# First expert's turned rows from an early gather of five token tiles and one-hot products for the other three

## The reference

```
x   = x + merged @ w_out
h2  = rms_norm(x, norm2_g)
gl  = h2 @ w_gr + b_gr                     # 4 groups
el  = h2 @ w_er + b_er                     # 4 x 8 experts
g   = argmax(gl);  top 2 of the 8 experts of group g
w   = softmax(top 2 logits) * softmax(gl)[g]
out = x + sum over the token's two experts of w * ((silu(h2 @ w_gate) * (h2 @ w_up)) @ w_down)
```

## Time and profile before

| | us |
|---|---|
| three runs, median (lowest to highest) | 1482.31 (1481.53 to 1482.49) |
| the profiled execution, its own time | 1481.47 |
| its span in the profile | 1479.7 |
| TensorE busy | 1424.3 (96%) |
| VectorE busy | 1008.1 (68%) |
| ScalarE busy | 828.9 (56%) |
| GpSimd busy | 407.7 (28%) |
| mean of a weight piece's high half on ScalarE | 1.907 |
| mean of a weight piece's low half on VectorE | 2.285 |

### The profile page before, as it was taken

The page is one execution under the profiler, slowest core; times in us unless marked ns, Lnnn a source line. Parts: engine busy times, 40 slices in busy tenths (PEclk is TensorE's granted clock), DMA queues, the critical chain, the costliest instruction groups (busy, mean ns, idle before and its releaser), DMA issues.

```text
span 1479.7 us, 19519 instructions
## 1 busy us (share of the span) xinstructions
PE 1424.3 (96%) x7296; PEld 1199.5 (81%) x7297; DVE 1008.1 (68%) x1444; ACT 828.9 (56%) x1342; POOL 407.7 (28%) x462
## 2 busy tenths in 40 slices
PE   5899999999999999999999979999999999999996
PEld 5788888888888788888888867888888888888885
DVE  6855664664574533344332567999999999999996
ACT  5653453353353322233232227888888888888883
POOL 3225424424433400000000011233333333333331
PEclk9999999999999999999999988999999999999999
DMA  7010110210210143354330549999999999999992
GB/s 220 23 44 12 51 44 1 62 43 1 61 44 0 44 115 99 86 149 121 91 142 36 198 152 385 375 386 385 392 386 387 386 389 389 393 396 393 389 384 89
DMA packets 134032, 286.39 MB, mean 194 GB/s; under 512 B 18864, under 2 KB 97840, under 8 KB 109360
## 3 DMA queue, kind: packets, MB, share of 16 engines
q1 hardware_dynamic: 119216, 263.79, 49.3%
q0 software_dynamic: 13248, 21.00, 3.8%
q10 hardware_dynamic: 1472, 0.32, 0.1%
HBM read 287.16 MB, written 25.17 MB: 211 GB/s over the span
## 4 chain that ended last, share of the span: by engine, by line
PE 85%; DMA 4%; DVE 4%; ACT 2%; POOL 2%; issue 2%; POOLq 0%; DVEq 0%; ACTq 0%
PE proj L105 17%; PE proj L107 16%; PE proj L106 16%; PE scores L105 6%; PE scores L107 6%; PE scores L106 6%; DMA w_slot<-in_w_up 4%; PE outs L760 2%; PE scores L693 2%; PE scores L571 1%; PE turned L105 1%; PE turned L107 1%; PE turned L106 1%; PE outs L851 1%; DVE w_low L1747 1%
## 5 line engine op out<-in xcount | busy, mean ns | idle before, releaser
L1747 DVE TENSOR_TENSOR w_low<-w_slot,w_high 128x2048 fp32r<-128x2048 f32 x192 | 430.9, 2285 | 0.1
L1186 ACT ACTIVATE w_high<-w_slot 128x2048 fp32r<-128x2048 f32 x190 | 352.6, 1907 | 20.1 <-DMA w_slot<-in_w_up 8.5
L105 PE MATMUL proj<-w_high,xeH 128*128 128x512 f32 x512 | 203.8, 398 | 3.9 <-DVE xeL L1850 1.9
L107 PE MATMUL proj<-w_high,xeL 128*128 128x512 f32 x512 | 200.6, 392 | 0.0
L106 PE MATMUL proj<-w_low,xeH 128*128 128x512 f32 x512 | 200.1, 391 | 0.0
L1376 POOL DMA_INDIRECT out<-y,ids_rows x31 | 86.5, 2791 | 342.8 <-DVE y L1860 342.8
L999 ACT ACTIVATE wCH<-wC_in 128x1024 fp32r<-128x1024 f32 x48 | 47.6, 1052 | 154.1 <-DMA wC_in<-in_w_branch_b 154.1
L1442 DVE TENSOR_TENSOR wCL<-wC_in,wCH 128x1024 fp32r<-128x1024 f32 x48 | 56.9, 1237 | 92.3 <-ACT wCH L999 92.3
L105 PEld LDWEIGHTS proj<-w_high,xeH 128*128 128x128 f32 x512 | 97.0, 189 | 25.5 <-issue 3.7
L107 PEld LDWEIGHTS proj<-w_high,xeL 128*128 128x128 f32 x512 | 96.5, 188 | 20.9
L106 PEld LDWEIGHTS proj<-w_low,xeH 128*128 128x128 f32 x512 | 96.7, 189 | 19.2
(11 more groups left out here) (299 smaller groups left out, 3167.4 us busy)
## 6 DMA issues: line engine op xcount, KB each, us to landing
w_slot<-in_w_gate SPq DMA_DIRECT2D x64, 1024.0 KB, 11.1
w_slot<-in_w_up SPq DMA_DIRECT2D x64, 1024.0 KB, 11.2
w_slot<-in_w_down SPq DMA_DIRECT2D x64, 1024.0 KB, 11.7
wC_in<-in_w_in SPq DMA_DIRECT2D x32, 512.0 KB, 4.8
wB_in<-in_w_in SPq DMA_DIRECT2D x16, 512.0 KB, 6.1
wA_in<-in_w_in SPq DMA_DIRECT2D x12, 512.0 KB, 5.9
x_all<-in_x SPq DMA_DIRECT2D x4, 1024.0 KB, 8.8
wC_in<-in_w_branch_a SPq DMA_DIRECT2D x16, 256.0 KB, 5.7
```

What stands on the lines that cost most here:

```text
L105: pe.matmul(out, lh, rh, start=start, stop=False)
L107: return pe.matmul(out, ll, rh, start=False, stop=stop)
L1186: act.activation(w_high[slot][:], w_in6[slot][:], ACT.Copy).then_inc(S["w_split"], 1)
L1747: dve.tensor_tensor(w_low[slot][:], w_in6[slot][:], w_high[slot][:].bitcast(F32), ALU.subtract).then_inc(S["w_lows"], 1)
```

## The change

Tiles 0 to 4 are "early" (`N_EARLY = 5`).

- The row table of tiles 0 to 4 is closed by itself and gives `first_ids`; GpSimd gathers expert 0's rows of these tiles into `xe[1]`, in its list ahead of the norm factor of tile 6. `rows_of(4)` moves ahead of the last piece of `out_proj(15)`.
- For tiles 5 to 7 VectorE makes a one-hot row for expert 0 alone (`first_hot`), and TensorE multiplies x2 with it. These products and products of the gathered rows with the identity add up in the banks 6 and 5, in which the turned rows of expert 0 then stand. They are interleaved with the last routing jobs.
- VectorE, not ScalarE, scales the turned rows; the high and low halves of the first four blocks are made one block at a time.
- The picks and row products of tiles 5 to 7 and the table `ids_rows` come later: the row products behind the first quarter of expert 0's gate and up. The gather of all of expert 0's rows (for the norm and the residual) and that of expert 1 follow this table.
- SP loads pieces 4 to 7 after the early gather has landed (`xe_landed1`), and 8 and on after the turned rows and all stores.
- Piece 2's high half is made by ScalarE after half tile 11, its low half by VectorE in iteration 4, in the projection stage.
- `top_group` is one step shorter; VectorE's places of tile 5 stand ahead of the last residual; the last result's scatter waits for one count instead of two; some waits on stores are merged.

```
 SP
-            sp.wait_ge(S["xe_landed0"], DMA)
+            sp.wait_ge(S["xe_landed1"], DMA)
             for q in range(4, 6 * N_EXP):
                 if q == 8:
-                    sp.wait_ge(S["x2_stored"], N_TILES * DMA)
-                    sp.wait_ge(S["out_stored"], N_TILES * DMA)
+                    sp.wait_ge(S["x0_T"], 2)
+                    sp.wait_ge(S["early_stored"], 2 * N_EARLY * DMA)
+                    sp.wait_ge(S["late_stored"], 2 * (N_TILES - N_EARLY) * DMA)
...
 TensorE, after out_proj(15)
+            def first_late(t, ks):
+                pe.wait_ge(S["place_step"], FIRST_HOT[t])
+                for k in ks:
+                    last = pe.matmul(first_turned(k), x2[:, t, DS(k, 128, step=8)], first_pick[t - N_EARLY][:, :],
+                                     start=(t == N_EARLY and k % 4 == 0), stop=(t == N_TILES - 1 and k % 4 == 3))
+                return last
+            def first_early(ks):
+                pe.wait_ge(S["xe_landed1"], DMA)
+                for k in ks:
+                    pe.matmul(first_turned(k), xe[1][:, DS(k, 128, step=8)], ident, start=False, stop=False)
+            first_late(5, range(4))
             turn_half(15)
+            first_late(5, range(4, 7))
+            positions_of(6)
             route_half(15)
-            positions_of(6)
-            rows_of(5)
+            first_early(range(4))
+            first_late(6, range(4))
+            first_late(5, [7])
+            first_early(range(4, 8))
             positions_of(7)
-            rows_of(6)
-            rows_of(7)
...
+            first_late(6, range(4, 6))
+            first_late(7, range(4)).then_inc(S["x0_T"], 1)
+            first_late(6, range(6, 8))
+            first_late(7, range(4, 8)).then_inc(S["x0_T"], 1)
...
 TensorE, run_gate_up
+                    if e == 0 and c == 1:
+                        pe.wait_ge(S["xs_done"], 8)
...
+                    if e == 0 and c == 0:
+                        last_rows()
...
 ScalarE
-                if cnt in (9, 10):
+                if cnt in (9, 10, 11):
                     high(w_high[cnt - 9][:], w_in6[cnt - 9][:], S[f"w_land{cnt - 9}"], DMA, S["w_split"])
...
-            high_piece(2)
+            act.wait_ge(S["xs_done"], 4)
+            for k in range(4):
+                act.activation(xeH[:, k, :], xs[:, k, :], ACT.Copy).then_inc(S["x0_H"], 1)
+            act.wait_ge(S["xs_done"], 8)
+            act.wait_ge(S["route_step"], R_DIFFS)
+            act.activation(xeH[:, 4:8, :], xs[:, 4:8, :], ACT.Copy).then_inc(S["xeH_done"], 1)
             high_piece(3)
...
 GpSimd, norm factors
             for i in range(N_TILES):
+                if i == N_EARLY + 1:
+                    pool.wait_ge(S["xe_zero"], 1)
+                    pool.wait_ge(S["early_stored"], 2 * N_EARLY * DMA)
+                    pool.wait_ge(S["tables_done"], 1)
+                    pool.indirect_dma_start(out=xe[1][:], ...
                 pool.wait_ge(S["n2_sq"], 9 + i)
...
 VectorE
             for i in range(N_TILES):
                 if i >= 1:
                     top_group(i - 1)
+                if i == 7:
+                    first_hot(5)
+                    place_rows(5)
                 add_residual(1, i)
...
-                if i >= 2:
+                if 2 <= i < 7:
                     place_rows(i - 2)
-                if i in (2, 3):
+                if i == 6:
+                    dve.wait_ge(S["rows_mm"], N_EARLY)
+                    route(dve.tensor_scalar(w_rows[:, 0:32], bank(3)[:, 0:32], float(NO_ROW), None, ALU.add))
+                    row_ids(first_ids[:], bank(3)[:, 0:1], "tables_done")
+                if i in (2, 3, 4):
                     low_piece(i - 2)
+            first_hot(6)
+            place_rows(6)
             top_group(7)
             two_experts(7)
-            place_rows(6)
+            first_hot(7)
             place_rows(7)
...
+            first_scaled(0)
+            for k in range(4):
+                dve.wait_ge(S["x0_H"], k + 1)
+                dve.tensor_tensor(xeL[:, k, :], xs[:, k, :], xeH[:, k, :].bitcast(F32), ALU.subtract).then_inc(S["x0_L"], 1)
+            for t in range(N_EARLY, N_TILES):
+                pick_rows(t)
+            first_scaled(1)
             route(dve.tensor_tensor(gdiff[:], ...
             route(dve.tensor_tensor(vdiff[:], ...
+            dve.wait_ge(S["xeH_done"], 1)
+            dve.tensor_tensor(xeL[:, 4:8, :], xs[:, 4:8, :], xeH[:, 4:8, :].bitcast(F32), ALU.subtract).then_inc(S["xeL_done"], 1)
+            dve.wait_ge(S["rows_mm"], 8)
+            dve.tensor_tensor(ids_rows[:, 0:32], bank(3)[:, 32:64], w_rows[:, 0:32], ALU.add).then_inc(S["tables_done"], 1)
```

More of the change, by code:

```diff
@@ L38 @@
 N_GROUPS = 4
+NO_SLOT = 4096.0
+N_EARLY = 5
+PLACED = {t: 2 * t + 2 + max(t - N_EARLY + 1, 0) for t in range(N_TILES)}
+FIRST_HOT = {t: PLACED[t] - 2 for t in range(N_EARLY, N_TILES)}
 def expert_at(j):
@@ L269, in decoder_layer @@
         gtop = rt("gtop", [P, 1])
-        gneg = rt("gneg", [P, 4])
+        far = rt("far", [P, 3])
+        first_ids = rt("first_ids", [P, 1], I32)
         el = rt("el", [P, 4, 8])
@@ L305, in decoder_layer @@
         r_rows = rs("r_rows", [P, 256])
+        first_pick = [sb(f"first_pick{i}", [P, 128], F32, at=R_WORK + 16 * KIB + (i + 1) * KIB + 512) for i in range(3)]
         rc = region(merged_at[1] + 16 * KIB, merged_at[1] + 16 * KIB + 1152)
@@ L372, in bank, with pos_bank @@
             return [PROJ[0], PROJ[1], TB, OB][n - 4][:, :]
+        def pos_bank(t):
+            return bank(2 if t <= N_EARLY else t - N_EARLY - 1)
         def x_bank(i, half):
@@ L534, in store_x2 @@
                 sp.wait_ge(S["x2_done"], 9 + i)
-                sp.dma_start(x2_v[:, i, :], x2[:, i, :]).then_inc(S["x2_stored"], DMA)
-                sp.dma_start(out_v[:, i, :], x2[:, i, :]).then_inc(S["out_stored"], DMA)
+                done = "early_stored" if i < N_EARLY else "late_stored"
+                sp.dma_start(x2_v[:, i, :], x2[:, i, :]).then_inc(S[done], DMA)
+                sp.dma_start(out_v[:, i, :], x2[:, i, :]).then_inc(S[done], DMA)
             for i in range(4):
@@ L951, in last_down @@
                     last.then_inc(S["w_used"], 1)
-            pe.wait_ge(S["xe_landed0"], DMA)
-            for half, done in ((0, "x0_T"), (1, "xeT_done")):
-                for k in range(4 * half, 4 * half + 4):
-                    last = pe.transpose(SC[:, 0, k * 128:(k + 1) * 128], xe[0][:, DS(k, 128, step=8)], ident)
-                last.then_inc(S[done], 1)
             for e in range(N_EXP):
@@ L1221, in _ @@
             act.wait_ge(S["xe_landed0"], DMA)
+            act.wait_ge(S["rows_mm"], 9)
             act.activation(first_sq[:], xe[0][:], ACT.Square, scale=1.0 / 32, accum_out=first_ms[:]).then_inc(S["first_sum"], 1)
[L1223 to L1228 removed]
             for c in (0, 1):
@@ L1747, in low_piece, with row_ids, first_scaled @@
                 dve.tensor_tensor(w_low[slot][:], w_in6[slot][:], w_high[slot][:].bitcast(F32), ALU.subtract).then_inc(S["w_lows"], 1)
+            def row_ids(table, rows, done):
+                dve.tensor_scalar(table, rows, float(NO_ROW), None, ALU.add).then_inc(S[done], 1)
+            def first_scaled(half):
+                ks = slice(4 * half, 4 * half + 4)
+                dve.wait_ge(S["x0_T"], half + 1)
+                dve.tensor_tensor(xs[:, ks, :], bank(6 - half).rearrange("p (k c) -> p k c", k=4),
+                                  g2x[:, ks].unsqueeze(2).to_broadcast([P, 4, 128]), ALU.mult).then_inc(S["xs_done"], 4)
             for i in range(N_TILES):
@@ L1844, in hid_low @@
                                   high_[:].rearrange("p a b -> p (a b)").bitcast(F32), ALU.subtract).then_inc(S["hidL_done"], 1)
-            low_piece(2)
-            for half, ready, done in ((0, "x0_H", "x0_L"), (1, "xeH_done", "xeL_done")):
-                dve.wait_ge(S[ready], 1)
-                ks = slice(4 * half, 4 * half + 4)
-                dve.tensor_tensor(xeL[:, ks, :], xs[:, ks, :], xeH[:, ks, :].bitcast(F32), ALU.subtract).then_inc(S[done], 1)
             low_piece(3)
@@ L1865, in last_rows @@
                 dve.wait_ge(S[f"again_landed{e % 2}"], DMA * ((e - N_GROUPS) // 2 + 1))
-                for half, done in ((0, "y_half"), (1, "y_out")):
+                for half in range(2):
                     cols = slice(half * 512, half * 512 + 512)
```

122 lines of the change are left out of this document (67 added, 55 removed).

## The result

| | kernel before | changed kernel |
|---|---|---|
| four runs each on one chip, median, us | 1482.4 | 1492.82 |
| lowest to highest | 1481.53 to 1482.73 | 1491.63 to 1496.89 |
| profiled execution, its own time | 1481.47 | 1492.83 |
| its span | 1479.7 | 1490.6 |

The ratio is 1.0071, with a 95% interval of 1.0059 to 1.0084. The change costs 10.4 us. The forecast was 1484.3 and its range ended at 1489.5: the sign of the likeliest case was right, its size was a fifth of what came.

A forecast was written before the change was run, and what follows sets the result against it. TensorE and the weight stream both run full; the end is set by expert 1's start plus 2.8 us of a late weight stream. +3.3 (the +1.0 in it) - 1.3 = +2.0 us gave 1484.3, range 1478.0 to 1489.5.

The forecast's parts named there:

- Piece 2, +1.0: Projection: ScalarE's split of piece 2 after half tile 11 delays TensorE and everything behind by 1.0 us, bounds 0 and 1.5.
- The norm held, residual at 877.7: GpSimd issues the early gather before tile 6's norm, so the last residual starts at 877.7 instead of 872.62, +5.1 us.
- Rival (d): Tile 6's norm is not held: early gather cheap for GpSimd, residual only 3 us late; total 1482.3, chance 0.15.
- The clock back at 881: Hand-over: TensorE's granted clock falls as before but is full again from 881, as work is nearly without gaps.
- rival (c): The clock does not rise in the burst of small products, everything behind 4.8 us later; total 1489.1, slower, chance 0.16.
- 64 instructions at 0.115 us: TensorE's new products for expert 0: 0.115 us per instruction at full clock, 0.245 at half; first expert product at 889.0.
- Gathers of 8.7 and 10.8 us, issued 1.6 apart: Full gathers under weight-stream load: expert 0's rows land at 903.2, expert 1's, issued 1.6 us later, at 906.9.
- rival (a): The gathers land as on an idle queue, in 4.7 us, the second about one later; total 1479.5, chance 0.14.
- Expert 1 at 913.8: After the hand-over, expert 1's first product starts at 913.8, 3.3 us later than at 910.47.
- Starvation, -1.3: End of the expert loop: an earlier weight stream gives back 1.3 of 2.8 us lost to late pieces, bounds 0 and 2.8.
- Sum: Whole kernel: +3.3 (the +1.0 is in it) - 1.3 = +2.0 us, giving 1484.3 against the median 1482.31.
- Rival (b): The first expert's gain is kept: expert 1's turn starts at 900.7, 4.0 earlier, and starvation goes; total 1476.3, chance 0.08.

## Why the prediction was wrong, step by step
- *Piece 2, +1.0.* Wrong: it cost TensorE nothing. The router product is at 855.73 instead of 854.55, but the one ahead of it is as late already; they are 7.32 us apart, 7.30 before. The piece landed 6.4 us after its issue, not 7.3, and the copy of half tile 12 was done at 855.56, just ahead of the product. The version without this split confirms it. This is the lower bound that the prediction gave (0, if the piece lands earlier).
- *The norm held, residual at 877.7.* Right in kind: rstd at 874.60, residual at 877.61. The hit on the number is luck: the trace is 1.2 us late, in place of the 1.0 of piece 2 that never came, and the hold itself moved the residual by 3.8 us. Rival (d) is out all the same.
- *The clock back at 881.* Right; rival (c), the slower case, is out, although the time came out beyond its 1489.1.
- *64 instructions at 0.115 us.* **This is the step that failed.** At full clock they cost 0.24. The first product came at 894.57 instead of 889.0 and the table at 898.17 instead of 893.6. The price was read from turns and from table products: the first have the distance but are no products, the second are products but have no distance. With the distance taken out the table comes 5.9 us earlier, and all points of the forecast up to expert 1's start are met within 1.3 us.
- *Gathers of 8.7 and 10.8 us, issued 1.6 apart.* The landings were 10.0 and 10.6: the row taken was the right kind, and rival (a) is refuted by these; its 4.7 us exist only with the stream held. But the issue of the first took 2.80 us, not 1.3, so the second went out 3.1 us behind it: +1.5.
- *Expert 1 at 913.8.* It was 920.37. The 6.6 us are 4.6 from the table, 1.5 from the issue and 0.5 from the weighing (5.31 us, most of it at half clock).
- *Starvation, -1.3.* Wrong in sign: +1.0. The forecast took the lead to be improvable by an earlier stream. Only pieces 4 to 7 went out early (880.46 on); the next came at 894.84, against 890.13 before. In 915 to 933 a piece landed a median 7.8 us after its issue (8.2 before), in 1020 to 1060 it was 8.6 (7.8), and by 1350 to 1375 it is 17.6 in both. The wait taken out gave nothing either. From turn to turn the loop takes 17.77 us an expert in both kernels until the last four; the difference lies in these. Why isn't settled: in versions without the hold the rest is 569.4 to 570.9 us, against 569.2.
- *Sum.* +3.3 -1.3 became +9.9 +1.0, of which 1.2 is the late profile. Rival (b), the gain kept, is out: expert 0 had no gain to keep, and where it has one (888.50 with neighbouring columns) the table behind the first scaling eats it, as argued. It stayed eaten until table and gathers were moved too.

## What to carry to other kernels
Price a float32 product by a row with the same kind of instruction and the same distance between its columns, on both operands: here 8 bytes were free, and 16 or more doubled it. An early transfer that splits a gather in two helps only if what still needs the whole list is not pushed behind the new work; here the table and its gathers, which nobody named as the goal, set the end. A transfer that lands in 5 us on a quiet queue took 9 to 11 once the weight stream ran. Holding the stream for it helped, but 0.7 to 2.2 us came back here, and most of that was the clock: TensorE's idle time moved to just ahead of expert 1's products, 1.5 us went to products at half clock, and only the shorter chain behind the gather won them back. Last, before a shift of one us is put down to an edit, see whether the trace is late already where both kernels do the same.

## What the runs showed of the hardware
- The step between 8 and 16 bytes: loads of 192, 197, 327 and 335 ns at 4, 8, 16 and 32 bytes, and 0.21 to 0.24 us from product to product where the spread operand is the streamed one; turns free of it at 32 bytes (189 ns).
- The issue of an indirect gather on GpSimd took 1.0 to 1.3 us with no low half beside it (902.35 and 872.97 in the changed kernel). Begun while VectorE's low half of a piece ran (two operands and the result in SBUF), it ended 0.9 us after that had ended: at 902.05 in the changed kernel, low half until 901.12 (2.80 us); at 896.59 with neighbouring columns, low half until 895.72 (1.85). Begun just ahead of the low half it was no longer than alone: 1.06 us (893.37, low half from 893.43), and 1.32 in the kernel before (883.27, low half from 883.40). These go together in the traces that were read; no run changed the one alone.
- A first full gather under the weight stream landed 8.6 to 9.0 us after the start of its issue where the issue took 1.05 us, and 10.0 to 10.8 where it took 2.80: most of the spread is the issue. With the stream held it was 4.3 to 5.8 with the short issue and 6.1 with the long one.
- A wait of 2.2 us of TensorE ahead of expert 1's products was followed by a fall of the granted clock to 0.50, and products 0.43 us apart; behind a wait of 0.48 us it stayed at 1.00.
